# Third layer's attention on one core: probabilities scaled on GpSimd, outputs split on VectorE

## The reference, cut to what matters

```python
s = jnp.einsum('qgrd,qkgd->qgrk', q_blk, k_sel, preferred_element_type=jnp.float32) * scale
s = jnp.where(valid[:, None, None, :], s, -jnp.inf)
p = jax.nn.softmax(s, axis=-1).astype(v_s.dtype)
return jnp.einsum('qgrk,qkgd->qgrd', p, v_sel)
...
return o.reshape(B, T, A_Q_W) @ w_out
```

## Time and profile before

| | |
|---|---|
| median of 3 runs (lowest to highest) | 1279.21 us (1278.23 to 1280.11) |
| the profiled execution's own time | 1279.56 us |
| its span, first to last instruction | 1277.8 us |
| PE busy in the span | 1251.1 us (98%) |
| DVE, ACT, POOL busy | 800.9 us (63%), 732.6 us (57%), 366.7 us (29%) |
| mean granted TensorE clock | 0.995 |
| chain that ended last | PE 93%, DVE 3%, ACT 2% |

### The profile page before, as it was taken

One profiled execution on the slowest core, in us unless ns is written; L12 is line 12 of the kernel. 1 busy time (PEld: TensorE's weight loads), 2 busy tenths in 40 slices (PEclk: granted clock), 3 DMA queues, 4 the chain that ended last, 5 costly groups with the idle time before them and its releaser, 6 DMA issues.

```text
span 1277.8 us, 28120 instructions
## 1 busy us (share of the span) xinstructions
PE 1251.1 (98%) x10218; PEld 1205.8 (94%) x10218; DVE 800.9 (63%) x1417; ACT 732.6 (57%) x1368; POOL 366.7 (29%) x413
## 2 busy tenths in 40 slices
PE   6999999999999999999989899999999999999999
PEld 6988999999988999999969599999999889999999
DVE  5687755556576755556689975554547666755444
ACT  6476666654455566666547854443436776544433
POOL 2011344411000144431123127770100220677100
PEclk9999999999999999999989899999999999999999
DMA  7542665666665466566545055555556443656665
GB/s 262 181 127 83 194 189 182 187 206 205 204 186 158 139 190 188 180 193 212 166 144 168 6 162 181 170 179 182 179 167 187 147 139 102 194 182 184 197 189 155
DMA packets 65766, 218.76 MB, mean 171 GB/s; under 512 B 9152, under 2 KB 13456, under 8 KB 65552
## 3 DMA queue, kind: packets, MB, share of 16 engines
q1 hardware_dynamic: 63344, 210.99, 53.5%
q10 hardware_dynamic: 2336, 6.58, 1.7%
HBM read 214.04 MB, written 1.08 MB: 168 GB/s over the span
## 4 chain that ended last, share of the span: by engine, by line
PE 93%; DVE 3%; ACT 2%; issue 1%; DMA 1%; SPq 0%; ACTq 0%; DVEq 0%
PE bank L344 28%; PE bank L346 27%; PE bank L345 27%; DVE wlo L328 1%; PE bank L933 1%; PE bank L918 1%; PE bank L915 1%; PE bank L1167 1%; ACT prob L971 1%; PE bank L358 1%; PE bank L840 0%; ACT whi L323 0%; DVE ulo L412 0%; PE bank L360 0%; PE bank L359 0%
## 5 line engine op out<-in xcount | busy, mean ns | idle before, releaser
L328 DVE TENSOR_TENSOR wlo<-raw,whi 128x1024 fp32r<-128x1024 f32 (+1 forms) x391 | 479.6, 1227 | 163.2 <-ACT whi L323 162.3
L344 PE MATMUL bank<-uhi,whi 128*128 128x256 f32 (+1 forms) x1824 | 527.5, 289 | 16.6 <-DVE wlo L328 10.7
L346 PE MATMUL bank<-uhi,wlo 128*128 128x256 f32 (+1 forms) x1824 | 519.8, 285 | 0.0
L345 PE MATMUL bank<-ulo,whi 128*128 128x256 f32 (+1 forms) x1824 | 519.3, 285 | 0.0
L323 ACT ACTIVATE whi<-raw 128x1024 fp32r<-128x1024 f32 (+1 forms) x391 | 407.6, 1045 | 184.4 <-PE bank L346 175.4
L344 PEld LDWEIGHTS bank<-uhi,whi 128*128 128x128 f32 x1824 | 347.0, 190 | 25.0 <-issue 22.1
L346 PEld LDWEIGHTS bank<-uhi,wlo 128*128 128x128 f32 x1824 | 347.3, 190 | 0.0
L345 PEld LDWEIGHTS bank<-ulo,whi 128*128 128x128 f32 x1824 | 346.0, 190 | 0.5
L344 PE MATMUL bank<-ahi,whi 128*128 128x256 f32 (+1 forms) x1168 | 333.3, 285 | 0.4 <-DVE wlo L328 0.4
L346 PE MATMUL bank<-ahi,wlo 128*128 128x256 f32 (+1 forms) x1168 | 331.1, 283 | 0.0
L345 PE MATMUL bank<-alo,whi 128*128 128x256 f32 (+1 forms) x1168 | 330.8, 283 | 0.0
(11 more groups left out here) (287 smaller groups left out, 1220.1 us busy)
## 6 DMA issues: line engine op xcount, KB each, us to landing
raw<-stream SPq DMA_DIRECT2D x391, 512.0 KB, 4.1
scratch<-decay ACTq DMA_DIRECT2D x8, 416.0 KB, 4.0
scratch<-relh ACTq DMA_DIRECT2D x8, 384.0 KB, 3.5
scratch<-scratch SPq DMA_DIRECT2D x60, 34.0 KB, 2.4
constants<-consts SPq DMA_DIRECT2D x1, 1300.0 KB, 11.3
h<-xT SPq DMA_DIRECT2D x4, 256.0 KB, 5.7
out<-h SPq DMA_DIRECT2D x8, 128.0 KB, 3.5
scratch<-scratch SPq DMA_DIRECT2D x16, 16.0 KB, 3.1
```

The lines of the kernel that those rows point to most:

```text
L328: dve.tensor_tensor(wlo[:, s, 0:w], raw[:, s, 0:w], whi[:, s, 0:w].bitcast(F32), ALU.subtract).then_inc(w_lo, 1)
L344: pe.matmul(dst, hi, a, start=first and i == 0, stop=False)
L345: pe.matmul(dst, hi, b, start=False, stop=False)
L346: mm = pe.matmul(dst, lo, a, start=False, stop=last and i == chunks - 1)
```

## The change

- DVE no longer multiplies the third layer's probabilities. `recip_dve` makes the reciprocals of both heads of a pair in one instruction and adds one to a new semaphore, `r_ready`.
- POOL does the four multiplications of each pair (`scale_pool`), after all that it had in `dsa_pool`. The instruction is `tensor_scalar` with two multiplications, by the reciprocal and by 1.0. `p_norm` counts as before.
- DVE makes `ahi` as well, straight ahead of `alo` (`out_split_dve`), one iteration earlier than `out_lo` had stood: out_split(s-2) comes in iteration s behind the reciprocals of s-1. ACT's `out_hi` is gone from this layer. The other two attention layers with this softmax keep `scale_dve` and `out_hi`.

```diff
+        r_ready = sem("r_ready")
...
+        def recip_dve(dve, s):
+            i = 2 * s % dsa.n
+            dve.wait_ge(p_exp, 2 * (dsa.head0 + 2 * s + 2))
+            dve.reciprocal(dsa.rinv[:, i:i + 2, :], dsa.ssum[:, i:i + 2, :]).then_inc(r_ready, 1)
+
+        def scale_pool(pool, s):
+            a = dsa
+            pool.wait_ge(r_ready, s + 1)
+            for i in (2 * s, 2 * s + 1):
+                for t, (c0, w) in enumerate(((0, a.w0), (a.w0, a.w1))):
+                    x = a.bufs[i % a.n][:, c0:c0 + w]
+                    pool.tensor_scalar(x, x, a.rinv[:, i % a.n, t:t + 1], 1.0, ALU.mult, ALU.mult).then_inc(p_norm, 1)
+
+        def out_split_dve(dve, s):
+            pr = dsa.head0 // 2 + s
+            dve.wait_ge(o_ready, pr + 1)
+            dve.tensor_copy(ahi[:, s, 0:256], dsa.obank[:, 0:256]).then_inc(o_hi, 1)
+            out_lo(dve, dsa, s)
...
 (dsa_act)
-            for s in range(1, 10):
+            for s in range(1, 9):
...
-                if s >= 2:
-                    out_hi(act, a, s - 2)
...
 (dsa_dve)
-                if 3 <= s <= 8:
-                    out_lo(dve, a, s - 3)
                 if 1 <= s <= 8:
-                    pair_scale_dve(dve, link, a, s - 1)
+                    recip_dve(dve, s - 1)
+                if 2 <= s <= 8:
+                    out_split_dve(dve, s - 2)
...
-                if s >= 8:
-                    out_lo(dve, a, s - 2)
+                if s == 9:
+                    out_split_dve(dve, 7)
...
 (dsa_pool)
             add(len(units) - 2)
             add(len(units) - 1)
             gather(1)
+            for s in range(dsa.pairs):
+                scale_pool(pool, s)
```

## The result

| | before | after |
|---|---|---|
| median of 8 runs (lowest to highest) | 1278.67 us (1277.22 to 1280.11) | 1281.40 us (1280.40 to 1283.39) |
| ratio, 95% interval | | 1.0024 [1.0014, 1.0034] |
| the profiled execution's own time | 1279.56 us | 1281.22 us |
| its span, mean granted clock | 1277.8 us, 0.995 | 1279.3 us, 0.995 |
| first maximum (m0) to values of pair 0, 1, 6, 7 | 7.69, 11.54, 28.57, 36.28 us | 9.69, 13.98, 31.89, 39.91 us |

The change costs 2.7 us, 0.24%. At pair 7 the stage is 3.6 us longer.

What follows compares the result with a forecast made beforehand. The prediction took DVE, at 3.00 us an iteration, to bound the attention loop. A start 1.85 us later plus six iterations at 3.19 us gave +3.0 us on the median of 1279.21: 1282.2 us, range 1279.6 to 1285.2.

Steps and rivals of the forecast that it cites:

- ring: Third layer's attention loop: reciprocals, POOL, transposes, scores, values, output split, maxima in a cycle; 6.38 us per two iterations, 3.19 against 3.00 each.
- Fast POOL: Rival on POOL's scaling: fixed 0.17 us plus the memset's 0.83 ns a column, W = 1.34, +1.35, 1280.6 us; chance 0.14.
- POOL's price: Cost of POOL's multiplications, which no profile row had, bracketed from memset, copy and two-input rows: 1.03 to 2.38 us a pair.
- W: POOL's time for the four multiplications of one pair, taken as 1.75 us.
- The start: First pair of the loop: POOL scales only after its additions and gather, so transposes come W + 0.1 = 1.85 us later.
- the tail's extra steps: Work in the loop beyond six times DVE's 3.00 us an iteration, taken as the same before and after.
- Part 3, hidden: Last pair's scaling, copies and values lie beside 6 us of PE products; ACT's missing out_hi gains nothing: no change.
- The sum: Later start plus six longer iterations: 4 W - 4.0 = +3.0 us at W = 1.75.
- Relief counts: Rival in the loop: a shorter ring leaves ACT as bound, 2.7 to 2.9 us an iteration, 1279.2 us; 0.12, of which 0.06 faster.
- Slow POOL: Rival: multiplications cost as much as two-input operations or more, POOL held up beside DVE; from +5.5 us, 1284.7; chance 0.16.

Runs made afterwards that it cites:

- e4_pair0_dve: Changed kernel, but DVE scales pair 0 and POOL begins with pair 1; 1279.95 us, 1.0012 against before.
- e1_pool_only: Changed kernel, POOL still scaling, but the output split given back as before: ACT the high part, DVE the low part; 1280.58 us, 1.0017 against before.
- e3_recip_first: Changed kernel with DVE's reciprocals of pair s-1 moved ahead of the maxima of pair s; 1279.72 us, 1.0008 against before.
- e11_pool_256_twice: Changed kernel with only POOL's 256-column multiplications made twice; 1287.07 us, 1.0070 against before.
- e10_weights_first: Changed kernel with DVE's high and low part of pair 6's outputs moved behind the two splits of weights; 1281.29 us, 1.0025 against before.
- e9: Changed kernel with reciprocals ahead of maxima, pairs 0 and 7 scaled by DVE, pair 6's output split behind the weight splits; 1278.06 us, 0.9991 against before.
- e12: The same kernel as e9, measured again in more rounds; 1277.79 us, 0.9994 against before.
- e8: e1_pool_only with pairs 0 and 7 scaled by DVE, so POOL scales pairs 1 to 6 only; 1278.10 us, 0.9991 against before.
- e7: Changed kernel with every POOL multiplication made twice, the first result into an unused area; 1292.23 us, 1.0110 against before.
- e2: Changed kernel, but DVE scales as before and also makes the high part, POOL does no scaling; 1280.40 us, 1.0011 against before.

## Why the prediction was right

The forecast was 1282.2 us (1279.6 to 1285.2), most likely slower by over 0.2%; the runs gave 1281.4 and 1.0024. The mechanism, a later start and a ring, is what the runs show. The number owes something to luck: it was slower by over 0.2% by a thin margin, and it lies as near to the rival *Fast POOL* (1280.6) as to the forecast. By the steps:

- **POOL's price.** W = 1.75 was taken from a bracket of 1.03 to 2.38; it is 1.62. The price per column is the memset's (0.83 ns) and the fixed part, 0.27 us, is larger than that of either neighbour, 0.10 and 0.17. *Fast POOL* had the column's price right and the fixed part too small (1.34). The middle of a bracket so wide was a guess, and that it came within 0.13 was luck. The Trainium skill, "GPSIMD Engine Reference", section "Engine selection", has one-input operations at roughly line rate. The row agrees as far as it goes: 0.83 ns a column is no more than the memset's, which reads nothing. The rule leaves out the fixed 0.27 us, which is over half of each multiplication here.
- **The start, W + 0.1 = 1.85.** The transposes moved by 1.88 and the values of pair 0 by 2.00. `e4_pair0_dve` gives all of it back.
- **The ring.** 6.38 us for two iterations were predicted, 6.34 measured, with POOL 0.13 shorter and the second transposes 0.10 longer. `e1_pool_only` (high part away from DVE) and `e3_recip_first` (reciprocals ahead of the maxima) break it in two places, and each makes the loop shorter than before's; `e11_pool_256_twice` shows W once in two steps. From pair 1 to pair 6 the loop is 0.88 us longer, where five times 0.19 is 0.95. That holds for the sum only: the five steps changed by +0.74, -0.10, +0.21, -0.44 and +0.47. The prediction took the tail's extra steps as the same before and after; they are the same in sum (17.03 - 5 x 3.00 = 2.03 and 17.91 - 5 x 3.17 = 2.06), but fall into other steps, since in after some lie on the ring. Pair 0 to pair 6 is 1.32 longer against 1.1; step 0-1 has the other 0.44, and PE was at half clock for 3.0 of its 4.3 us, in before for 2.3 of 3.9.
- **Part 3, hidden, was wrong by 0.3 us.** POOL's and ACT's share of it held. But the high part of pair 6 on DVE stands ahead of the splits of weights, and the end grew by 0.31, which `e10_weights_first` gives back.
- **The sum.** 4W - 4.0 is +2.5 at the measured W; the stage's +3.6 is that plus 0.3 at the start, 0.6 in the loop (mostly its first step) and 0.3 at the end. The medians differ by 2.7. Two errors offset each other: W too large, and these extras left out. Why the medians differ by 0.9 less than the two profiled stages isn't settled; two executions of one kernel, `e9` and `e12`, differ by 1.05 in the stage itself.
- **The rivals.** *Relief counts* fell, though DVE was relieved just as said (10.14 to 7.50 us of 11): the relief was of an engine that then had to wait. Its premise, a shorter ring, came true only where the ring was opened, in `e1_pool_only`, `e3_recip_first` and the kernels built on them. *Fast POOL* fell by its premise and not by its time: W is 1.62, nearer to 1.75 than to 1.34. *Slow POOL* fell in the changed kernel, but its mechanism is real and shows in `e1_pool_only`, 3.64 us for 1.62; in the changed kernel POOL's pair 7 (733.91, 1.62 us) was finished at 735.53, before the splits began at 737.01.

## What to carry to other kernels

Relieving an engine that is 92 to 97% busy gains only if what leaves it doesn't come back as a wait in its own program order: add up one turn of the ring, and compare it with the busy time that goes. If a step moves to a helper engine, issue what starts the helper ahead of long work that needs nothing from it; here that one line was worth 2 us of an 18 us loop. The first and the last item of a pipeline deserve a decision of their own, since the helper's latency lies bare at the start, and at the end it may meet other work.

## What the runs showed of the hardware

- A `tensor_scalar` on POOL with a scalar for each row took 372 ns for 128 x 128 and 478 ns for 128 x 256 float32: doubling the columns costs 28%. The two parts of a head have reciprocals of their own, so the fixed 0.27 us was paid 32 times.
- Four of them took 3.64 us in place of 1.62 beside DVE's subtractions of two SBUF tiles, all of it in one that waited (2387 ns for 372), and DVE's took no longer (2.38 us against 2.35). Beside DVE's maxima and outputs, which read a bank, the groups took 1.62 to 1.64 us; the longest others, 1.68 to 1.77, stood beside the tail's scaling on DVE, which reads only SBUF.
- Waiting can cost more than its own length. Where PE was busy for 1.87 to 2.07 us of 4 (`e8` from 706, `e7` from 720 and 732), the granted clock stood in the next 4 us at 0.50 to 0.58, and in `e7` a pair's scores of 128 columns took PE 0.80 us where they took 0.49 in the loop of after. `e7`'s stage has 3.27 us more than 4W gives, and its two turns at half clock are longer by just that. It isn't a certain consequence: in `e2` PE was busy for 1.85 us of 706 to 710, less than in `e8`, and in `e11` for 2.61 us of 730 to 734, and in both the clock was 1.00 in the stretch behind it.
